# Expert rows of items 0 to 6 kept in DRAM and fetched by token, operand's high part first in five projections, the double norm ordered by norms, the experts' end rotated

## The chip, the cores and the metric

The kernel runs on one core of one Trainium2 chip. The metric is the device time of one execution in microseconds (us). PE is the matmul engine, PEld its weight load, DVE, ACT and POOL the vector, scalar and GpSimd engines, SP the queue that loads the weights.

## The reference, cut to what matters

Three blocks run over 256 tokens of width 1024, all in float32.

```python
def first_block(x, ...):
    h = rmsnorm(x, norm_mix_pre)
    y = mixer(h, w_in, ..., w_out)            # gated conv and gated linear attention
    x = x + rmsnorm(y, norm_mix_post)
    h = rmsnorm(x, norm_ffn_pre)
    y = conv_mlp(h, w_up, conv_ffn, w_down)
    return x + rmsnorm(y, norm_ffn_post)

def moe_swiglu(x, router_w, router_b, w_gate_up, w_down):
    logits = jnp.einsum('td,de->te', xf, router_w) + router_b
    top_v, top_i = lax.top_k(logits, TOP_K)                     # 2 of 8
    gates = jax.nn.softmax(top_v, axis=-1)
    combine = jnp.sum(gates[..., None] * jax.nn.one_hot(top_i, N_EXPERTS), axis=1)
    y = jnp.zeros(xf.shape, F32)
    for e in range(N_EXPERTS):
        y = y + combine[:, e:e + 1] * swiglu(xf, w_gate_up[e], w_down[e])
    return y

def second_block(x, p, ...):
    for i in range(2):
        h = fox_sb_mixer(x, ...) if i == 0 else swa_mixer(x, ...)
        x = layer_norm(DEEPNORM_ALPHA * x + h, ln_mix_g[i], ln_mix_b[i])
        h = swiglu(x, ...) if i == 0 else moe_swiglu(x, ...)
        x = layer_norm(DEEPNORM_ALPHA * x + h, ln_ffn_g[i], ln_ffn_b[i])
        x = x + jax.nn.sigmoid(x @ ple_w_gate[i]) * (p[i] @ ple_w_proj[i])
    return x
```

## The kernel before

**Tiling.** The 256 tokens are two tiles of 128, kept in SBUF as x[tile] of 128x1024. Each projection turns its input first: eight 128x128 transposes for each tile on PE (turn_tile, L2032) into PSUM, of which ACT copies a rounded high part xt_hi (turned, L636) and DVE makes the remainder xt_lo (L1146, rows of L1150). Weights come in chunks of 1 MB, 128x2048, on SP's queue (load, L395) into a ring of raw slots, four of them and during the experts six (w_raw and raw_more). ACT rounds a chunk to w_hi (round_chunk L613, rounds L1049; all of ACT's copies have the line L611), DVE subtracts to w_lo (split_chunk L1138, splits L1701). PE then makes three products for each piece: high by high, the other two with one low part each. A 128x512 product takes some 0.23 us from start to start.

**What sets the order.** Each engine's program is written out by hand: pool from L470, act from L605, dve from L1129, pe from L1905. Engines meet at semaphores. An engine executes in order, so a wait holds whatever is written behind it.

**Operands.** operand(m, src) (L2040) puts in keep_warm products (bf16 of no use, L1998, rows of L2001; BEFORE and BETWEEN at L2003 to L2004 give their numbers), turns tile 0, more warmers, turns tile 1, seven warmers and waits for both tiles' xt_lo (xt_ready). m is 2 for w_up, 3 for ab_in, 5 for ffn_up, 7 for qkv, 9 for the router. The first chunk after it is cols_chunk (L1964, rows of L1976 to L1979) or rows_chunk (L1909, L1922 to L1924); the router's logits are L2575 to L2577.

**The double norm.** After w_out, DVE's rms_after (L1198) makes x of a tile from the projection, and rms_before (L1190) y of the tile from x for w_up's operand; ACT's squares (L678) and square_x (L693) deliver the sums of squares and the roots. The order is tile 0 both, then tile 1 both.

**The sliding-window attention's end.** DVE copies turned probabilities (COPY pt, L1449) that PE multiplies by v (L2413 to L2415), and splits c_out's chunks between.

**Experts.** The router puts up to 128 rows of an expert into an item; eight items run and up to three overflow items for what is left (If blocks on n_items). An item (L1056 ACT, L1724 DVE, L2489 PE) is 28 up-chunks in seven turns of a loop over j, each with four chunks, 48 products and a turn of the hidden rows mh, and 16 down-chunks in two halves: 504 products of 128x512. The rows xg of the next item are prepared beside: DVE's select (L1703) makes sel, the one-hot matrix of tokens against slots, PE turns it (turn_sel, L2471, with the gates' sum of L2476), and the row sum gives row_of (L1745), by which POOL fetches xr from x_rows in DRAM (fetch, L585); PE turns xr in the down part. The item's result, scaled by the gate, is split to ys_hi (ACT) and ys_lo (DVE, L1759), and in the next item PE multiplies it by the turned sel (scatter, L2479, rows of L2485: eight products), so that every row comes to its token, and DVE adds both tiles to y (added, L1713). After the last item come seven warmers, the scatter of the last result, the overflow branches and ple(1): its projection of p (ppt, 24 products for a block), then the norm of y and the turn of x (add_last, L1887), and the gate projection by tiles.

Of the kernel before, what the change touches and what calls it, by code (L numbers as in the profile page):

```python
# [14 lines left out]
ALU = mybir.AluOpType  # L15
ACT = mybir.ActivationFunctionType
F32 = mybir.dt.float32
# [95 lines left out]
MOE_CHUNKS = MOE_UP_CHUNKS + 2 * len(MOE_DOWN)  # L113


def build(nc, a, out, upto="end"):
# [27 lines left out]
    with ExitStack() as ctx:  # L144
# [29 lines left out]
        def S(name):  # L174
# [29 lines left out]
        route_i = sb("route_i", [P, 4], I32)  # L204
        row_of = sb("row_of", [P, 1], U32)
        tok_col = sb("tok_col", [P, NT])
        x_rows = nc.dram_tensor("x_rows", (SEQ + 1, D), F32, kind="Internal").ap()
        at_xt = free[0]
# [54 lines left out]
            ("selt", [P, SEQ], F32R), ("gslot", [P, 1], F32))  # L263
# [21 lines left out]
        def p_bank(i):  # L285

            return psum[:, 2 * (phase["c_out"][0][0] % 2), :] if i else scr[:, 3, :]
# [31 lines left out]
        def last_raw(k, n_items):  # L319
# [3 lines left out]
            return raw_order[at], 16 * (uses - N_EXP * uses_in_item(at)) + 16 * uses_in_item(at) * n_items  # L323
# [64 lines left out]
        def _(sp):  # L388
# [19 lines left out]
            if "moe" in live:  # L408
# [34 lines left out]
                if "ple1" in live:  # L443
                    for _, cc, n0, n, ps in phase["ple1"]:
                        for k, (k0, nk, m) in enumerate(ps, cc):
                            slot, _ = last_raw(k, n_items)
# [23 lines left out]
        def _(pool):  # L470
# [105 lines left out]
            if "moe" in live:  # L576
# [6 lines left out]
                pool.dma_start(x_rows[SEQ:SEQ + 1, :], xr[0:1, :]).then_inc(S("zero_stored"), 16)  # L583

                def fetch(i):  # L585

                    pool.wait_ge(S("row_ready"), i + 1)
# [3 lines left out]
                pool.wait_ge(S("zero_stored"), 16)  # L591
# [13 lines left out]
        def _(act):  # L605
# [7 lines left out]
            def round_chunk(k, r, n):  # L613

                slot, landed = (k % RING, 16 * (k // RING + 1) + 16 * r) if k < N_BEFORE_MOE else last_raw(k, n_items)
# [166 lines left out]
            for t in squares("w_out"):  # L782
                if t == 1:
                    for j in range(2):
                        turned(2, j)
                root_tile(t)
                square_x(t, y, lambda t: act.wait_ge(S("x_tile"), t + 1))
                root_tile(t)

# [160 lines left out]
            def ple(i, m, r=0):  # L950
# [12 lines left out]
                if i:  # L963
                    round_to(blocks[0][1] + RING, r)
                    for block_ in blocks[0:2]:
                        projected(*block_)
                    turned(m, 0)
                    turned(m, 1)
                    root_tile(1)
# [86 lines left out]
            def item(i):  # L1056
                c0, r = N_BEFORE_MOE, i * R_ITEM
                for j in range(MOE_PAIRS):
# [9 lines left out]
                    if j == 2:  # L1068
# [21 lines left out]
            if "moe" in live:  # L1090
# [19 lines left out]
                for i in range(1, N_EXP):  # L1110
                    item(i)
# [1539 lines left out]
```

## Time and profile before

| | us |
|---|---|
| median of 3 runs | 1875.41 (1875.24 to 1876.05) |
| the profiled execution, its own time | 1876.83 |
| span of its profile | 1874.7 |
| PE busy | 1827.1 (97%), 9840 matmuls |
| DVE, ACT busy | 1388.8 (74%), 1105.0 (59%) |
| mean granted clock of PE | 0.991 |

Busy time is the time in which an engine has an instruction under way; matmuls overlap, so a busy PE says that it has something to do, and the distance between two starts says how fast. The granted clock is given as a share of 2.4 GHz, and 0.50 is 1.2 GHz. A bracket behind a row of a timeline gives the idle time before it and what ended it.

### The profile page before, as it was taken

What the parts mean: (1) busy time and instruction counts of PE and PEld (TensorE: products, weight loads), DVE (VectorE), ACT (ScalarE), POOL (GpSimd) and SP (SyncE); (2) the same over time, 40 slices, a digit from 0 to 9 for tenths busy, and PEclk for the clock granted to TensorE, in tenths of its full rate; (3) what the DMA queues carried; (4) which work ended last, traced back from release to release, by engine and by line L of the source; (5) the groups of instructions that cost most, each with busy time, mean ns of one, the idle gap of its engine ahead of it and who ended that gap; (6) DMA issues with size and microseconds to landing.
All of it is one profiled execution on the core that took longest, in us unless ns stands there. A gap on an engine that the chain in (4) does not pass through costs nothing.

```text
span 1874.7 us, 24092 instructions
## 1 busy us (share of the span) xinstructions
PE 1827.1 (97%) x9840; PEld 1527.8 (81%) x9849; DVE 1388.8 (74%) x1200; ACT 1105.0 (59%) x989; POOL 61.6 (3%) x83
## 2 busy tenths in 40 slices
PE   8999999999999999999999999999999999999997
PEld 6979997897899877768788888888888888888875
DVE  4766775456655565689988888888888888888876
ACT  4544554364343344367766676767666767676672
POOL 2200000200000001000000000000000000000000
PEclk8999999999999999999999999999999999999998
DMA  7444546432555563259999999999999999999980
GB/s 252 158 153 157 179 157 213 141 131 100 176 179 179 179 203 136 69 205 384 339 381 361 338 368 352 362 356 342 377 361 340 366 355 362 356 342 379 357 308 24
DMA packets 248857, 491.02 MB, mean 262 GB/s; under 512 B 10423, under 2 KB 15611, under 8 KB 248753
## 3 DMA queue, kind: packets, MB, share of 16 engines
q1 hardware_dynamic: 244992, 477.30, 72.0%
q0 software_dynamic: 3328, 10.73, 1.7%
q8 instruction: 69, 1.13, 0.3%
q10 hardware_dynamic: 432, 1.57, 0.2%
q14 instruction: 36, 0.29, 0.0%
HBM read 487.46 MB, written 2.10 MB: 261 GB/s over the span
## 4 chain that ended last, share of the span: by engine, by line
PE 87%; DVE 7%; ACT 2%; issue 1%; DVEq 1%; DMA 0%; ACTq 0%; SPq 0%
PE psum L2511 17%; PE psum L2513 17%; PE psum L2512 17%; PE psum L1976 5%; PE psum L1979 5%; PE psum L1978 5%; PE psum L1922 5%; PE psum L1923 5%; PE psum L1924 5%; PE psum L1996 3%; DVE w_lo L1138 2%; ACT w_hi L611 1%; DVE w_lo L1701 1%; DVE uv L1398 1%; PE psum L2485 1%
## 5 line engine op out<-in xcount | busy, mean ns | idle before, releaser
L611 ACT ACTIVATE w_hi<-w_raw 128x2048 fp32r<-128x2048 f32 (+1 forms) x357 | 641.4, 1834 | 106.7 <-PE psum L1924 60.3
L1701 DVE TENSOR_TENSOR w_lo<-w_raw,w_hi 128x2048 fp32r<-128x2048 f32 (+1 forms) x238 | 511.3, 2187 | 75.2 <-ACT w_hi L611 75.0
L1138 DVE TENSOR_TENSOR w_lo<-w_raw,w_hi 128x2048 fp32r<-128x2048 f32 (+2 forms) x119 | 261.3, 2227 | 138.9 <-ACT w_hi L611 137.5
L2511 PE MATMUL psum<-w_hi,xg_hi 128*128 128x512 f32 x892 | 357.7, 401 | 1.3 <-DVE w_lo L1701 1.3
L2513 PE MATMUL psum<-w_hi,xg_lo 128*128 128x512 f32 x892 | 353.5, 396 | 0.0
L2512 PE MATMUL psum<-w_lo,xg_hi 128*128 128x512 f32 x892 | 353.5, 396 | 0.0
L1701 DVE TENSOR_TENSOR w_lo<-raw_more,w_hi 128x2048 fp32r<-128x2048 f32 (+1 forms) x118 | 254.5, 2195 | 35.2 <-ACT w_hi L611 35.0
L1976 PE MATMUL psum<-xt_hi,w_hi 128*128 128x256 f32 (+1 forms) x976 | 277.0, 284 | 0.7 <-DVE w_lo L1138 0.7
L1978 PE MATMUL psum<-xt_lo,w_hi 128*128 128x256 f32 (+1 forms) x976 | 274.8, 282 | 0.0
L1979 PE MATMUL psum<-xt_hi,w_lo 128*128 128x256 f32 (+1 forms) x976 | 274.8, 282 | 0.0
L611 ACT ACTIVATE w_hi<-raw_more 128x2048 fp32r<-128x2048 f32 (+1 forms) x118 | 212.7, 1838 | 19.0 <-PE psum L2513 18.5
L2511 PEld LDWEIGHTS psum<-w_hi,xg_hi 128*128 128x128 f32 x892 | 168.1, 188 | 40.9 <-DVE w_lo L1701 2.2
L2513 PEld LDWEIGHTS psum<-w_hi,xg_lo 128*128 128x128 f32 x892 | 167.9, 188 | 40.8
L2512 PEld LDWEIGHTS psum<-w_lo,xg_hi 128*128 128x128 f32 x892 | 168.2, 189 | 38.5
L1976 PEld LDWEIGHTS psum<-xt_hi,w_hi 128*128 128x128 f32 (+1 forms) x976 | 181.8, 186 | 3.5 <-DVE w_lo L1138 1.5
L1978 PEld LDWEIGHTS psum<-xt_lo,w_hi 128*128 128x128 f32 (+1 forms) x976 | 182.6, 187 | 0.5
L1979 PEld LDWEIGHTS psum<-xt_hi,w_lo 128*128 128x128 f32 (+1 forms) x976 | 182.6, 187 | 0.3
L2511 PE MATMUL psum<-w_hi,mh_hi 128*128 128x512 f32 x448 | 179.1, 400 | 0.0
L2513 PE MATMUL psum<-w_hi,mh_lo 128*128 128x512 f32 x448 | 177.6, 397 | 0.0
L2512 PE MATMUL psum<-w_lo,mh_hi 128*128 128x512 f32 x448 | 177.4, 396 | 0.0
L611 ACT ACTIVATE mg<-psum 128x512 f32<-128x512 f32 x56 | 33.6, 599 | 176.1 <-PE psum L2513 176.1
L1922 PE MATMUL psum<-w_hi,xt_hi 128*128 128x512 f32 (+1 forms) x256 | 104.5, 408 | 5.2 <-DVE xt_lo L1150 3.7
(395 smaller groups left out, 2122.9 us busy)
## 6 DMA issues: line engine op xcount, KB each, us to landing
w_raw<-in_moe_w_gate_up SPq DMA_DIRECT2D x150, 1024.0 KB, 7.8
raw_more<-in_moe_w_gate_up SPq DMA_DIRECT2D x74, 1024.0 KB, 7.7
w_raw<-in_moe_w_down SPq DMA_DIRECT2D x64, 1024.0 KB, 7.2
raw_more<-in_moe_w_down SPq DMA_DIRECT2D x32, 1024.0 KB, 7.5
w_raw<-in_w_up SPq DMA_DIRECT2D x22, 1024.0 KB, 5.4
w_raw<-in_ffn_w_gate_up SPq DMA_DIRECT2D x22, 1024.0 KB, 5.4
w_raw<-in_w_in SPq DMA_DIRECT2D x12, 1024.0 KB, 5.6
w_raw<-in_ab_w_in SPq DMA_DIRECT2D x12, 1024.0 KB, 5.2
```

The lines of the kernel that those rows point to most:

```text
L611: return act.activation(o, i, func, **kw)
L1138: TT(w_lo[:, k % RING, 0:n], raw(slot, n), w_hi[:, k % RING, 0:n].bitcast(F32), ALU.subtract)\
L1701: TT(w_lo[:, at, 0:n], raw(slot, n), w_hi[:, at, 0:n].bitcast(F32), ALU.subtract).then_inc(S("lo_ready"), 1)
L1922: mm(o, hi(k, t), wh, start=(k == ps[0][0]), stop=False)
L1923: mm(o, hi(k, t), wl, start=False, stop=False)
L1924: m = mm(o, lo(k, t), wh, start=False, stop=(k == kmax))
L1976: mm(o, w_hi[:, slot, cols], xt_hi[:, k, :], start=(k == 0 and c_ % 2 == 0), stop=False, skip_group_check=True)
L1978: mm(o, w_hi[:, slot, cols], xt_lo[:, k, :], start=False, stop=False, skip_group_check=True)
L1979: m = mm(o, w_lo[:, slot, cols], xt_hi[:, k, :], start=False, stop=(k == KD - 1), skip_group_check=True)
L2511: mm(o, hi[:, q, :], wh, start=(q == first), stop=False)
L2512: mm(o, hi[:, q, :], wl, start=False, stop=False)
L2513: m = mm(o, lo[:, q, :], wh, start=False, stop=(q == last))
```

## The change

1. **Stored rows.** The results of items 0 to 6 (STORED = 7) stay one float32 tile ys, which ACT scales by the gate, and POOL stores it to y_rows in DRAM. Their ys_lo, scatter, additions to y and (for items 1 to 6) the turn of sel are gone; the gate comes as a second column of the row sum. In item 0 DVE computes for each token the two places of its rows (rows_of_tokens); in item 7 POOL fetches them through xr, 512 KB for each tile and choice, and DVE adds them to y. Item 7 and overflow items are scattered as before, but by halves of the columns.
2. **The experts' end rotated.** An item is a head and an end (its last two roundings and the result's second half). The last item's end comes behind the overflow branches, together with ple1's first two chunks, now rounded and split at their true width of 1024; ple1's gate chunks are split behind the norm of the second tile, and the gate projection's first block takes the products with w_hi first (rows_high_first). Warmers before the scatter and before the gate projection are gone, as is the wait for y_added there.
3. **High part first.** At m = 2, 3, 5, 7 and 9 the first chunk starts when xt_hi is there and takes its xt_lo products last; operand puts two warmers there instead of seven and doesn't wait; BETWEEN of w_up is 5 instead of 14. To free the bank for this, p is turned into a free accumulator bank, and so are the logits.
4. **Double norm by norms.** x of both tiles, then y of both tiles, on DVE and ACT.
5. **Attention's end.** The split of one chunk goes from before the last COPY pt to behind it, the next one behind the rows of the last heads.

```diff
@@ POOL
+                def store(i):
+
+                    pool.wait_ge(S("ys_hi_ready"), 2 * i + 2)
+                    pool.dma_start(y_rows[i * P:(i + 1) * P, :], ys[:]).then_inc(S("zero_stored"), 16)
+
+                def fetch_results(g):
+
+                    pool.wait_ge(S("row_ready"), STORED + g)
+                    pool.indirect_dma_start(xr[:], None, y_rows[:], bass.IndirectOffsetOnAxis(ap=token_rows[:, g:g + 1], axis=0))\
+                        .then_inc(S("xr_landed"), 16)
...
-                for i in range(N_EXP):
+                for i in range(STORED):
                     fetch(i)
+                    store(i)
+                pool.wait_ge(S("zero_stored"), 32 + 16 * STORED)
+                pool.wait_ge(S("xr_turned"), STORED)
+                for g in range(2 * NT):
+                    fetch_results(g)
+                fetch(STORED)
@@ ACT
+                if 0 < i < STORED:
+                    act.wait_ge(S("row_ready"), i)
+                if 0 < i <= STORED:
+                    act.wait_ge(S("zero_stored"), 32 + 16 * i)
+                wait_used(act, c0 + end, r)
+                item_rows(i, 0)
+                rounds(end + 2, MOE_CHUNKS, i)
+
+            def item_rows(i, n):
+
+                to = ys if i < STORED else ys_hi
+                copy(to[:, n * NB:(n + 1) * NB], psum[:, 4 + n, :], scale=gslot[:, gate_col(i)]).then_inc(S("ys_hi_ready"), 1)
...
+            def last_end():
+
+                c0 = chunk0["ple1"]
+                round_to(c0 + 2, n_items * R_ITEM)
+                wait_used(act, N_BEFORE_MOE, n_items * R_ITEM)
+                item_rows(ITEMS, 1)
+                round_to(c0 + 4, n_items * R_ITEM)
@@ DVE
             for t in rms_after(1, "w_out", "x_tile"):
+                pass
+            for t in range(NT):
                 rms_before(t, 2)
...
                 swa_sink(1)
-                round_to(c_sw + 7)
                 for t in range(NT):
                     turned_at(8, t, 2 * t, scr[:, t, :])
                 turned_prob(7)
-                round_to(c_sw + 8)
+                round_to(c_sw + 7)
                 attended(1)
...
+                    if i == STORED and 1 <= j <= 4:
+                        add_results(j - 1)
+                    if first and j == MOE_PAIRS - 1:
+                        rows_of_tokens()
...
+            def add_results(g):
+
+                dve.wait_ge(S("xr_landed"), 16 * (STORED + g + 1))
+                TT(y[:, g // 2, :], y[:, g // 2, :], xr[:], ALU.add).then_inc(S("row_ready"), 1)
...
+                last_end()
+                added(n_items, 0)
+                dve.drain()
                 add_last(0)
                 normalize(0, 10, y)
                 add_last(1)
@@ PE
-            BETWEEN = (0, 4, 14, 9, 4, 13, 4, 2, 4, 11, 4)
+            BETWEEN = (0, 4, 5, 9, 4, 13, 4, 2, 4, 11, 4)
...
-                if m not in (6, 10):
-                    keep_warm(7, 3)
-                pe.wait_ge(S("xt_ready"), 4 * (m + 1))
+                keep_warm(2, 3)
...
+            def cols_chunk_high_first(bl, i, r, m_):
...
+                pe.wait_ge(S("xt_hi_ready"), 4 * m_ + (3 if k0 + nk <= 4 else 4))
+                for part in range(2):
+                    if part:
+                        pe.wait_ge(S("xt_ready"), 4 * (m_ + 1))
...
+                            if part:
+                                m = mm(o, w_hi[:, slot, cols], xt_lo[:, k, :], start=False, stop=(k == KD - 1), skip_group_check=True)
+                            else:
+                                mm(o, w_hi[:, slot, cols], xt_hi[:, k, :], start=(k == 0 and c_ % 2 == 0), stop=False,
+                                   skip_group_check=True)
+                                mm(o, w_lo[:, slot, cols], xt_hi[:, k, :], start=False, stop=False, skip_group_check=True)
...
+                high(0, 0)
+                high(1, 0)
+                turn_tile(m, src, 1)
+                low(0, 0)
+                pe.wait_ge(S("xt_ready"), 4 * m + 4)
+                high(0, 1)
+                high(1, 1)
+                low(0, 1).then_inc(S("w_used"), 1)
+                low(1, 0)
+                low(1, 1).then_inc(S("w_used"), 1)
...
-                        if h == 0 and j == 0 and not first and i != N_EXP:
-                            scatter(i)
+                        if h == 0 and j == 0 and i > STORED:
+                            scatter(i, 1)
...
-                keep_warm(7, 0)
-                scatter(N_EXP)
+                scatter(N_EXP, 0)
...
                 overflow(N_EXP)
+                scatter(n_items, 1)
```

What this does to the order of instructions is shown at three places. The first is PE in item 1, at the turn of the third pair's hidden rows; sel is the one-hot matrix. Before:

```order
L2512 MATMUL psum<-w_lo,xg_hi 128x512
L2513 MATMUL psum<-w_hi,xg_lo 128x512
L1996 MATMUL psum<-ident,mh 128x128 x4
L1996 MATMUL psum<-ident,sel 128x128 x2
L2476 MATMUL psum<-route,sel 128x1 x2
L2511 MATMUL psum<-w_hi,xg_hi 128x512
L2512 MATMUL psum<-w_lo,xg_hi 128x512
L2513 MATMUL psum<-w_hi,xg_lo 128x512
```

The change:

```order
L2712 MATMUL psum<-w_lo,xg_hi 128x512
L2713 MATMUL psum<-w_hi,xg_lo 128x512
L2165 MATMUL psum<-ident,mh 128x128 x4
L2711 MATMUL psum<-w_hi,xg_hi 128x512
L2712 MATMUL psum<-w_lo,xg_hi 128x512
L2713 MATMUL psum<-w_hi,xg_lo 128x512
```

The turn of sel and the gates' sum are gone in items 1 to 6, while the turn of mh stands. Item 1's scatter, before, stands like this on PE, behind the second chunk of the item, and nothing is left of it in the change:

```order
L2512 MATMUL psum<-w_lo,xg_hi 128x512
L2513 MATMUL psum<-w_hi,xg_lo 128x512
L2485 MATMUL psum<-ys_hi,selt 128x512
L2485 MATMUL psum<-ys_lo,selt 128x512
L2485 MATMUL psum<-ys_hi,selt 128x512
L2485 MATMUL psum<-ys_lo,selt 128x512
L2485 MATMUL psum<-ys_hi,selt 128x512
L2485 MATMUL psum<-ys_lo,selt 128x512
L2485 MATMUL psum<-ys_hi,selt 128x512
L2485 MATMUL psum<-ys_lo,selt 128x512
L2511 MATMUL psum<-w_hi,xg_hi 128x512
L2512 MATMUL psum<-w_lo,xg_hi 128x512
```

The second place is DVE at the experts' end, from the last item's chunks to the norm (raw_more and w_raw are raw slots, branches are the overflow's). Before:

```order
L1701 TENSOR_TENSOR w_lo<-raw_more,w_hi 128x2048 [waits hi_ready] x2
L1759 SCALAR_TENSOR_TENSOR ys_lo<-psum,gslot,ys_hi 128x512 [waits ys_hi_ready]
L1701 TENSOR_TENSOR w_lo<-w_raw,w_hi 128x2048 [waits hi_ready] x2
L1878 UNCONDITIONAL_BRANCH
L1715 REGISTER_ALU
L1716 TENSOR_TENSOR y<-y,psum 128x1024 [waits scattered]
L1892 BN_STATS bn<-y 128x6 x2
L1234 BN_AGGR stat<-bn 128x2 [waits gain_landed1,gain_landed0]
L1236 TENSOR_SCALAR stat<-stat 128x1
L1239 SCALAR_TENSOR_TENSOR x<-y,stat,gain 128x1024
L1178 RECIPROCAL stat<-stat 128x1 [waits root_ready]
L1241 SCALAR_TENSOR_TENSOR x<-x,stat,gain 128x1024
```

The change:

```order
L2008 UNCONDITIONAL_BRANCH
L1195 ISA
L1197 TENSOR_TENSOR w_lo<-raw_more,w_hi 128x1024 [waits hi_ready]
L1195 REGISTER_ALU
L1197 TENSOR_TENSOR w_lo<-raw_more,w_hi 128x1024 [waits hi_ready]
L1859 REGISTER_ALU
L1844 SCALAR_TENSOR_TENSOR ys_lo<-psum,gslot,ys_hi 128x512 [waits ys_hi_ready]
L1779 TENSOR_TENSOR y<-y,psum 128x512 [waits scattered]
L1779 TENSOR_TENSOR y<-y,psum 128x512
L1776 REGISTER_ALU
L1779 TENSOR_TENSOR y<-y,psum 128x512 [waits scattered]
L1790 BN_STATS bn<-y 128x6
```

Four splits of full width stood ahead of the addition of a whole tile; now two of half width and the result's second half do, behind the branches, and the additions are of 512 columns.

The third is DVE at the end of the sliding-window attention. Before:

```order
L1449 COPY pt_124<-psum 128x768 [waits at_t]
L1443 TENSOR_TENSOR smx_131<-smx_131,sink 128x16
L1138 TENSOR_TENSOR w_lo<-w_raw,w_hi 128x2048 [waits hi_ready]
L1157 TENSOR_TENSOR xt_lo<-psum,xt_hi 128x4x128 [waits xt_hi_ready] x2
L1449 COPY pt_124<-psum 128x768 [waits at_t]
L1138 TENSOR_TENSOR w_lo<-w_raw,w_hi 128x2048 [waits hi_ready]
L1455 TENSOR_TENSOR smx_131<-smx_131 128x16 [waits at_sum]
```

The change:

```order
L1510 COPY pt_125<-psum 128x768 [waits at_t]
L1504 TENSOR_TENSOR smx_132<-smx_132,sink 128x16
L1216 TENSOR_TENSOR xt_lo<-psum,xt_hi 128x4x128 [waits xt_hi_ready] x2
L1510 COPY pt_125<-psum 128x768 [waits at_t]
L1197 TENSOR_TENSOR w_lo<-w_raw,w_hi 128x2048 [waits hi_ready]
L1516 TENSOR_TENSOR smx_132<-smx_132 128x16 [waits at_sum]
L1518 RECIPROCAL smx_132<-smx_132 128x16
```

The copy of pt now has no w_lo between it and the one before.

## Rows read from the trace of the kernel before

**Rows 1.** The page, busy time and the chain.

```profile
PE 1827.1 (97%) x9840; PEld 1527.8 (81%) x9849; DVE 1388.8 (74%) x1200; ACT 1105.0 (59%) x989; POOL 61.6 (3%) x83
...
PE 87%; DVE 7%; ACT 2%; issue 1%; DVEq 1%; DMA 0%; ACTq 0%; SPq 0%
```

**Rows 2.** Tile views of row_of and of xr: duration ns min/median/max, first and last start.

```profile
L1745 DVE TENSOR_SCALAR row_of<-psum x8: 147/148/159, 892.0 to 1764.5; 128x1 uint32<-128x1 f32 x8
...
DMA to landing us min/median/max: 7.2/7.8/8.6
```

**Rows 3.** PE timeline at a scatter: start us, us, engine, line, op, [idle before <-releaser].

```profile
1078.55 0.40 PE L2485 MATMUL psum<-ys_hi,selt 128*128 128x512 f32 x1
...
1080.37 0.40 PE L2511 MATMUL psum<-w_hi,xg_hi 128*128 128x512 f32 x1
```

**Rows 4.** PE timeline at item 1's turn of sel.

```profile
978.81 0.38 PE L1996 MATMUL psum<-ident,sel 128*128 128x128 f32 x2
...
979.39 0.48 PE L2511 MATMUL psum<-w_hi,xg_hi 128*128 128x512 f32 x1
```

**Rows 5.** Windows: us, then busy us PE, PEld, DVE, ACT, POOL, PEclk, DMA share, GB/s.

```profile
830.00:880.00 50.00, 49.32 (x225) 39.75 (x224) 44.13 (x56) 36.32 (x29) 0.00 (x0) 1.00 1.05 387
1124.00:1249.00 125.00, 125.00 (x560) 101.16 (x559) 107.83 (x71) 87.61 (x64) 0.94 (x1) 1.00 1.00 358
```

**Rows 6.** The page, DMA issues: KB, median us to landing.

```profile
x_rows<-x ACTq DMA_DIRECT2D x2, 512.0 KB, 7.4
```

**Rows 7.** PE timeline at w_up's operand.

```profile
140.53 1.97 PE L1996 MATMUL psum<-ident,y 128*128 128x128 f32 x8 [2.65 <-DVEq L1196]
...
144.35 0.47 PE L1976 MATMUL psum<-xt_hi,w_hi 128*128 128x256 f32 x1
```

**Rows 8.** DVE timeline at w_out's double norm.

```profile
135.92 1.28 DVE L1218 SCALAR_TENSOR_TENSOR x<-y,stat,x 128x1024 f32<-128x1024 f32 x1
...
139.16 1.28 DVE L1195 SCALAR_TENSOR_TENSOR y<-x,stat,gain 128x1024 f32<-128x1024 f32 x1
```

**Rows 9.** PE timeline at ab_in's operand.

```profile
346.08 1.67 PE L2001 MATMUL psum<-ones_tri 128*128 128x512 bf16 x7
347.83 0.39 PE L1976 MATMUL psum<-xt_hi,w_hi 128*128 128x256 f32 x1
```

**Rows 10.** DVE and PE timelines at the sliding-window attention's end.

```profile
770.50 2.29 DVE L1138 TENSOR_TENSOR w_lo<-w_raw,w_hi 128x2048 fp32r<-128x2048 f32 x1
...
774.91 0.43 PE L2413 MATMUL psum<-p,pt 128*128 128x64 f32 x2 [2.34 <-DVE pt L1449]
...
782.31 0.60 PE L1996 MATMUL psum<-ident,y 128*128 128x128 f32 x4
```

**Rows 11.** PE and DVE timelines at the router.

```profile
808.38 1.09 PE L1996 MATMUL psum<-ident,x 128*128 128x128 f32 x8 [1.42 <-DVEq L1242]
...
811.99 2.29 DVE L1811 TENSOR_TENSOR xn_lo<-x,xn_hi 128x2048 fp32r<-128x2048 f32 x1 [0.17 <-ACT xn_hi L611]
814.95 0.17 DVE L1815 TENSOR_TENSOR route<-psum,rb_row 128x16 f32<-128x16 f32 x1 [0.67 <-PE psum L2581]
```

**Rows 12.** Windows with the granted clock at 0.50.

```profile
775.24:782.06 6.82, 6.82 (x22) 5.77 (x22) 3.54 (x5) 0.21 (x1) 0.92 (x1) 0.50 0.82 279
1836.78:1847.02 10.24, 4.87 (x15) 3.41 (x17) 9.21 (x16) 3.57 (x8) 0.00 (x0) 0.50 0.01 2
```

**Rows 13.** PE and DVE timelines of the experts' end and ple1.

```profile
1828.08 0.50 PE L1922 MATMUL psum<-w_hi,ppt_hi 128*128 128x512 f32 x1 [1.89 <-issue]
...
1833.56 0.39 PE L1924 MATMUL psum<-w_hi,ppt_lo 128*128 128x512 f32 x1
1841.93 1.97 PE L1996 MATMUL psum<-ident,x 128*128 128x128 f32 x8 [7.98 <-DVEq L1242]
...
1869.73 0.40 PE L1924 MATMUL psum<-w_hi,xt_lo 128*128 128x512 f32 x1
...
1835.88 1.22 DVE L1716 TENSOR_TENSOR y<-y,psum 128x1024 f32<-128x1024 f32 x1 [3.05 <-issue]
```

More of the change, by code:

```diff
@@ L1109, in _ @@
                 n_items = act.value_load(route_i[0:1, 3:4], min_val=N_EXP, max_val=ITEMS)
-                for i in range(1, N_EXP):
+                n_over = act.value_load(route_i[0:1, 4:5], min_val=0, max_val=ITEMS - N_EXP)
+                for i in range(1, N_EXP - 1):
                     item(i)
+                item_head(N_EXP - 1)
                 def overflow(i):
                     with act.If(n_items > i):
-                        item(i)
+                        item_end(i - 1)
+                        item_head(i)
                         if i + 1 < ITEMS:
@@ L1383, in _ @@
             for t in rms_after(1, "w_out", "x_tile"):
+                pass
+            for t in range(NT):
                 rms_before(t, 2)
@@ L1729, in item @@
                         lo_h(i, j - 1)
-                    elif not first:
+                    elif i > STORED:
                         scattered(i)
@@ L1885, in _ @@
                 me.cap = N_STATIC
[L1887 to L1892 removed]
+                last_end()
+                added(n_items, 0)
+                dve.drain()
                 add_last(0)
@@ L2471, in turn_sel @@
             def turn_sel(n):
-                for t in range(NT):
+                for t in range(NT if n else 0):
                     turn(psum[:, 4, t * P:(t + 1) * P], sel[:, t, :].bitcast(F32))
@@ L2477, in turn_sel, with scatter @@
                 m.then_inc(S("sel_turned"), 1)
-            def scatter(n):
-                pe.wait_ge(S("ys_ready"), 2 * n)
+            def scatter(n, h):
+                pe.wait_ge(S("ys_ready"), 2 * n - 1 + h)
                 for t in range(NT):
-                    for h in range(2):
-                        for q, part in enumerate((ys_hi, ys_lo)):
-                            m = mm(psum[:, 4 + 2 * t + h, :], selt[:, t * P:(t + 1) * P], part[:, h * NB:(h + 1) * NB],
-                                   start=(q == 0), stop=(q == 1))
-                    m.then_inc(S("scattered"), 1)
+                    for q, part in enumerate((ys_hi, ys_lo)):
+                        m = mm(psum[:, 4 + 2 * t + h, :], selt[:, t * P:(t + 1) * P], part[:, h * NB:(h + 1) * NB],
+                               start=(q == 0), stop=(q == 1))
+                m.then_inc(S("scattered"), 1)
             def item(i, first=False):
```

279 lines of the change are left out of this document (194 added, 85 removed).

## The prediction

> **What bounds the kernel now.** I read the page first: PE is busy for 1827.1 of the span's 1874.7 us, and 87% of the chain that ended last is PE's [rows 1]. So a matmul that disappears is worth its start-to-start distance, and work of other engines is worth nothing unless PE waits for it. Then the tile view of row_of and xr [rows 2]: one row_of per expert item, eight in all, from 892.0 to 1764.5, so an item takes (1764.5 - 892.0) / 7 = 124.64 us. Eight fetches also say that no overflow item runs. Next the windows: in a whole item PE is busy all 125 us, DVE 107.8, ACT 87.6 [rows 5]: PE sets the pace there. Last the timelines at the boundaries between stages, where PE does wait, and the windows in which the granted clock is 0.50, that is 1.2 GHz [rows 7 to 13].
>
> **Experts, rows stored.** In each of items 1 to 7 stand eight scatter products, in item 2 from 1078.55 to the next weight product at 1080.37 [rows 3]: 1.82 us. Before, seven of these stand inside the items (the eighth is in the tail, below): 7 x 1.82 = 12.7 us gone. The turn of sel with its gate products runs from 978.81 to 979.39 [rows 4], 0.58 us; items 1 to 6 lose it, 3.5 us, and item 0 loses its two turns, some 0.2. The row sum only gets a second column. Sum 16.4 us, all on the path, because PE has no idle time to fill there.
>
> What is added lies beside PE, if the others keep up:
> - **DVE** loses two ys_lo and two y additions in an item and gains twelve small operations in item 0 and four additions of 128x1024 in item 7. One such addition takes 1.22 us [rows 13]. A turn of the item's loop over four up-chunks has 48 products of some 0.24 us (24 ppt products run from 1828.08 to 1833.80, [rows 13]), 11.5 us, and DVE fills 107.8 / 125 = 86% of an item [rows 5], here 9.9: with 1.22 more it is at 11.1, so it fits with 0.4 us to spare. That is thin, and each addition waits for a fetch.
> - **The fetches** of item 7 go one after the other through xr: each takes 7.8 us to landing [rows 2] and about one more for its issue, against one addition every 11.5 us. They fit.
> - **DMA.** An item loads 44.04 MB of weights and 0.52 of rows, and now stores 0.52: 45.1 MB in 122.3 us is 369 GB/s; with four fetches for item 7's additions 386. The trace shows 358 in a whole item, which is just the demand (44.56 / 124.64), and 387 over the 50 us of 830 to 880, where the six slots are being filled [rows 5]. So 369 is inside what was seen and 386 at its edge. I charge 0.4 us for items 0 and 7 together and take 16.0; bounds 12 (item 7 short of data by 4 us) and 17.2 (the turn's pipeline refill also saved).
>
> The nearest rule against this: the Trainium skill, "DMA: Bandwidth & Descriptors", section "Where 436 GB/s comes from", says that for HBM to SBUF the HBM side, about 358 GB/s for a core, binds. By that the 45.1 MB need 126 us, items 1 to 7 get longer instead of shorter, and the total is some 1867. The trace disagrees with its 387 over 50 us.
>
> **Operand's high part first.** At w_up, ab_in, ffn_up, qkv and the router, five of seven warmers go, and the first products need only the turned high part. At ab_in the seven warmers stand between 346.08 and 347.83 [rows 9]: 5/7 of 1.75 is 1.25 us. The pieces at ffn_up and qkv read the same: 3 x 1.25 = 3.75 us. The two left are 0.5 us and the ACT copies of the turn end about when they do, so nothing new waits; bound below 0.6 each (ACT late), above 1.45. At the router the logits come 1.3 us earlier, but DVE's 2.29 us operation at 811.99 stands ahead of the step that reads them at 814.95 [rows 11], which can only start at 814.3: 0.65 us; bounds 0 and 1.3. w_up is in the next part.
>
> **Double norm by norms.** Before, tile 0's second norm (3.1 us with its wait for ACT) stands ahead of tile 1's first. x of tile 1 is ready at 135.92 + 1.28 = 137.2, y of tile 1 at 139.16 + 1.28 = 140.44, of which 1.96 is waiting for ACT's squares and root [rows 8]. Norm by norm x of tile 1 comes at about 133.8, ACT's squares of tile 0 are hidden under it, and the two y end at about 136.7 and 138.75. Tile 0's turn gets some 3 us later and tile 1's, which decides, 1.7 earlier (140.53 to 138.8) [rows 7]. PE then idles some 3 us before turn 0. Here the gap of 2.65 us before turn 1 was followed by a turn of 1.97 us, and one of 2.34 at 774.91 by the window at 0.50 [rows 7, 10, 12], so I take turn 1 and two warmers at half speed, 1.8 and 0.9 us: first product at 141.4 instead of 144.35. That is 3.0 us with the fewer warmers in it; bounds 2.0 (more products at half clock) and 4.3 (no fall).
>
> **End of the sliding-window attention.** DVE makes a 2.29 us w_lo at 770.50, ahead of the copy pt [rows 10]; PE waits 2.34 us for pt, and from 775.24 to 782.06 its clock is 0.50 [rows 10, 12]. Without that w_lo the copy waits for ACT's xt_hi instead, pt is ready 1.3 us earlier, PE's gap is 1.0 us; one of 1.42 at the router left the turn behind it at 1.09 us, full speed [rows 11]. The 18 small and 12 large products from 774.91 to 782.31 took 7.4 us; at full clock the 12 large ones take 12 x 0.24 = 2.8, the small ones 1.35, with the earlier start 773.6: y's turn at 777.75. The moved w_lo ends at 775.8 and y at about 777.7, so they don't hold it. Gain 4.6 us; 2.3 if the clock falls all the same.
>
> **Experts' end.** Before: the scatter's eight products end at 1826.2, behind seven warmers that now go; 1.89 us for the branches, 24 ppt products to 1833.8, while DVE works off four 2.2 us splits, waits and only adds at 1835.88; the turn of tile 0 is at 1841.93, after 7.98 us of idle PE; the last product starts at 1869.73 [rows 13]. After: the first half is scattered at 1822.4, straight behind the last expert product, and added under the branches, the second half at 1825.4, DVE adds it at 1826.45, having before it only two splits of half width. From DVE's addition to the turn it was 6.05 us, less 0.5 for the half addition: turn 0 at 1832.0, 9.9 us earlier, just where the ppt products now end. From that turn to the last product's end before: 28.0 us, five warmers and a turn at half clock among them. After, DVE's normalization of tile 1 ends at 1839.2 and the first w_lo at 1841.5; PE waits 2.5 us for the turned operand (1832.9 to 1835.4), does high products of tile 0, waits about 1.0 for w_lo: about 28.1 again. That is 9.8, and the 2.5 us gap is of the size that brought the clock down, for 6.8 us at 774 and for 10.2 in the tail before [rows 12]. A 6.8 us stretch costs up to 3.4 us: I take the middle, 8.1. Bounds 5 and 9.8.
>
> **Sum.** 16.0 + 3.75 + 0.65 + 3.0 + 4.6 + 8.1 = 36.1 us. The profiled execution took 1876.8, so 1840.7 for it; the median of the runs shown is 1875.41, 1.4 lower, and 1875.4 - 36.1 = **1839.3**. All low ends together: 12 + 1.8 + 0 + 2.0 + 2.3 + 5 = 23, 1852; all high ones: 17.2 + 4.35 + 1.3 + 4.3 + 4.6 + 9.8 = 41.6, 1834.
>
> **Rivals.**
> - *The warmers are missed.* Fourteen go at w_up and five at each other place, and PE has 1.0 to 2.5 us gaps with fewer products around. A stretch like 775.24 to 782.06 [rows 12] costs half of its 6.8 us; two or three of them 7 to 10: about 1848. Against: the gap of 1.42 us at the router wasn't followed by a fall [rows 11]. Chance 0.08.
> - *Item 7 starves, or DVE falls behind.* 386 GB/s, a serial chain of fetches, DVE with 0.4 us to spare: 5 to 10 us, 1844 to 1849. For: DVE's high share [rows 5]. Chance 0.09.
> - *Transfers can do no more than the 358 GB/s of the whole items*, whose DMA share is already 1.00 [rows 5]: 45.1 MB take 126.0 us, 3.7 more than planned, seven times: 26, so 1865. Against: the 387 (share 1.05) and that 358 equals the demand. (The Trainium skill's rule above would act like this.) Chance 0.05.
> - *The other side: each new transfer stops the weight stream.* If the weights stand still for the whole landing time of a store (7.4 us for 512 KB, [rows 6]) or fetch (7.8), 7 x 7.4 + 4 x 7.8 = 83 us: 1922. It decides for slower from (36.1 + 3.75) / 11 = 3.6 us of PE time per transfer. Against: today's fetch of xr takes 7.8 us in each item and PE has no idle time in it [rows 2, 5]. Chance 0.03.
> - *It doesn't do what it says*: a token beyond an expert's 128 rows would go the old way; eight fetches say there is none. With the stores' wait in front of ACT's copy of the next item's rows PE could stall, but a store has over 100 us. Chance 0.01, near 1856.
>
> **How the numbers follow.** The forecast's own mechanism has 0.74. The range holds its bounds and the first two rivals: 1832 (two below the high sum, for what I have not seen) to 1853; outside are the capped transfers, the blocked stream and the failed change, 0.09, and some 0.06 of misjudged sizes. What a measurement can tell from no change is 0.2%, 3.75 us, 1871.7 to 1879.2. Only the blocked stream lies above; a mild form of it lies within: faster 0.96, same 0.01, slower 0.03.
>
> **What would show it.** Row_of's pitch falls from 124.64 to 122.3 with PE busy all the time in a window of an item; ys stores land in under 10 us; no PE wait for DVE or ACT above 0.5 us in item 7; the 0.50 window at 775 is gone and one near 137 to 142 remains; at the experts' end no idle PE stands before turn 0, and 2.5 us behind it. A pitch that stays near 124.6, or weight loads landing later than 9 us, would make the prediction wrong; so would more than 43 us from the first ppt product to the span's end (now 1874.7 - 1828.1 = 46.6, forecast 40).

## The result and the profile after

The change takes 1828.19 us (median of 4, 1827.59 to 1830.17) against 1875.73 for the kernel before (4 runs), a ratio of 0.9747 with the 95% interval 0.973 to 0.9764. It is faster, as forecast, but by 47.5 us instead of 36.1, and below the range of 1832 to 1853. The profiled execution has a span of 1826.2.

The page of the changed kernel: busy time, granted clock, chain, and DMA issues (KB each, median us to landing).

```profile
PE 1783.6 (98%) x9701; PEld 1502.2 (82%) x9708; DVE 1369.5 (75%) x1198; ACT 1099.7 (60%) x976; POOL 73.7 (4%) x95
...
PEclk8999999999999999999999999999999999999999
...
PE 87%; DVE 7%; ACT 2%; issue 1%; DVEq 1%; DMA 0%; ACTq 0%; SPq 0%
...
w_raw<-in_moe_w_gate_up SPq DMA_DIRECT2D x150, 1024.0 KB, 9.1
```

The shape is that of [rows 1]: 98% busy PE, and PE has 87% of the chain. The same row of the kernel before:

```profile
w_raw<-in_moe_w_gate_up SPq DMA_DIRECT2D x150, 1024.0 KB, 7.8
```

So the weight loads land later, 9.1 us after issue instead of 7.8. The prediction had named more than 9 us as a sign of being wrong. It came, and nothing followed from it: in a whole item PE is busy all the time, with 373 GB/s where [rows 5] have 358.

```profile
1124.00:1249.00 125.00, 125.00 (x560) 101.58 (x560) 107.55 (x69) 87.13 (x62) 1.54 (x2) 1.00 1.01 373
138.03:141.44 3.41, 3.41 (x14) 2.30 (x13) 2.57 (x5) 1.21 (x3) 0.53 (x1) 0.50 0.33 108
1786.66:1790.08 3.42, 3.42 (x10) 2.67 (x9) 2.63 (x6) 1.98 (x3) 0.00 (x0) 0.50 0.04 16
```

(Columns as in [rows 5].) Only two stretches at 0.50, 1.2 GHz, are left between the start and the end, each 3.4 us: one at w_up's turn, one behind the branches at the experts' end. That is 6.8 us, where the kernel before has 23.9 us. The two of [rows 12] are gone. The item's pitch, from the tile view of row_of:

```profile
L1827 DVE TENSOR_SCALAR row_of<-psum x8: 148/152/159, 873.9 to 1726.4; 128x1 uint32<-128x1 f32 x8
```

(1726.4 - 873.9) / 7 = 121.79 us, where 122.3 was forecast. PE at w_up's operand, at the attention's end and at the experts' end:

```profile
136.66 1.09 PE L2165 MATMUL psum<-ident,y 128*128 128x128 f32 x8 [3.56 <-DVEq L1255]
...
139.28 1.91 PE L2165 MATMUL psum<-ident,y 128*128 128x128 f32 x8
...
141.46 0.47 PE L2125 MATMUL psum<-xt_hi,w_hi 128*128 128x256 f32 x1
```

```profile
761.49 0.43 PE L2613 MATMUL psum<-p,pt 128*128 128x64 f32 x2 [1.05 <-DVE pt L1510]
...
765.73 0.60 PE L2165 MATMUL psum<-ident,y 128*128 128x128 f32 x4
```

```profile
1785.74 0.49 PE L2685 MATMUL psum<-ys_hi,selt 128*128 128x512 f32 x1 [1.99 <-DVE ys_lo L1844]
...
1793.92 1.04 PE L2165 MATMUL psum<-ident,x 128*128 128x128 f32 x8
1796.61 0.49 PE L2513 MATMUL psum<-w_hi,xt_hi 128*128 128x512 f32 x1 [1.65 <-DVE xt_lo L1209]
...
1802.47 1.20 PE L2520 MATMUL psum<-w_lo,xt_hi 128*128 128x512 f32 x4 [1.01 <-DVE w_lo L1197]
...
1821.21 0.40 PE L2049 MATMUL psum<-w_hi,xt_lo 128*128 128x512 f32 x1
```

The first answers to [rows 7]: a gap of 3.56 us, turn 1 at half clock, the first product at 141.46, where 141.4 was forecast. The second answers to [rows 10]: the wait for pt is 1.05 us instead of 2.34. The third answers to [rows 13]: no wait before turn 0, then 1.65 and 1.01 us, where 2.5 and 1.0 were forecast.

So where do the missing 11 us lie? Landmarks of both traces (start times in us), how far the change is ahead at each, and how far the forecast's terms up to there would have it:

```
                       before    after     ahead   forecast
first w_up product     144.35    141.46     2.9      3.0
last w_down product    341.25    335.96     5.3      3.0
first ab_in product    347.83    341.30     6.5      4.3
first ffn_up product   487.25    478.74     8.5      5.5
last ffn_down product  675.66    665.25    10.4      5.5
y's turn, attention    782.31    765.73    16.6     11.4
first expert product   822.44    804.99    17.5     12.0
last expert product   1822.13   1782.43    39.7     28.0
last product          1869.73   1821.21    48.5     36.1
```

At the boundaries between stages the steps are near those of the forecast. The rest comes inside stages that nothing of the change touches: 1.9 us in ffn_up and ffn_down alone. There the products simply follow each other faster. The mean distance from one start to the next, over all weight products of a stage at full clock, is 0.2342 us before and 0.2328 after for 128x512, 0.1200 and 0.1188 for 128x256, from the first 100 us on. 128x512 products of ppt, the turned p, alone have 0.234 in both. All operands but ppt's lie behind the one new declaration in SBUF, token_rows, which moves them by 32 bytes.

### The profile page after: what moved, and what is told of

Its sections match the earlier page's. It is cut to its first block, busy times and chain, and to the rows that moved or that the text cites. A ratio compares the mean times of both kernels' runs of the same rounds, so it can differ in the third digit from the quotient of the medians.

```text
span 1826.2 us, 23845 instructions
## 1 busy us (share of the span) xinstructions
PE 1783.6 (98%) x9701; PEld 1502.2 (82%) x9708; DVE 1369.5 (75%) x1198; ACT 1099.7 (60%) x976; POOL 73.7 (4%) x95
## 4 chain that ended last, share of the span: by engine, by line
PE 87%; DVE 7%; ACT 2%; issue 1%; DVEq 1%; DMA 0%; ACTq 0%; SPq 0%
PE psum L2711 16%; PE psum L2713 16%; PE psum L2712 16%; PE psum L2047 5%; PE psum L2049 5%; PE psum L2048 5%; PE psum L2142 5%; PE psum L2144 4%; PE psum L2145 4%; PE psum L2165 3%; DVE w_lo L1197 2%; DVE w_lo L1762 1%; ACT w_hi L641 1%; PE psum L2125 1%; PE psum L2127 1%
## 5 line engine op out<-in xcount | busy, mean ns | idle before, releaser
L1197 DVE TENSOR_TENSOR w_lo<-w_raw,w_hi 128x2048 fp32r<-128x2048 f32 (+2 forms) x121 | 265.7, 2228 | 133.5 <-ACT w_hi L641 132.0
L1762 DVE TENSOR_TENSOR w_lo<-raw_more,w_hi 128x2048 fp32r<-128x2048 f32 (+1 forms) x116 | 250.1, 2195 | 35.6 <-ACT w_hi L641 35.4
L2142 PE MATMUL psum<-xt_hi,w_hi 128*128 128x256 f32 (+2 forms) x768 | 217.8, 284 | 1.0 <-DVE w_lo L1197 1.0
L2144 PE MATMUL psum<-xt_lo,w_hi 128*128 128x256 f32 (+2 forms) x768 | 216.7, 282 | 0.0
L2145 PE MATMUL psum<-xt_hi,w_lo 128*128 128x256 f32 (+2 forms) x768 | 216.6, 282 | 0.0
L2142 PEld LDWEIGHTS psum<-xt_hi,w_hi 128*128 128x128 f32 (+2 forms) x768 | 143.5, 187 | 3.2 <-DVE w_lo L1197 1.9
L2144 PEld LDWEIGHTS psum<-xt_lo,w_hi 128*128 128x128 f32 (+2 forms) x768 | 143.5, 187 | 0.5
L2145 PEld LDWEIGHTS psum<-xt_hi,w_lo 128*128 128x128 f32 (+2 forms) x768 | 143.5, 187 | 0.3
L2713 PEld LDWEIGHTS psum<-w_hi,mh_lo 128*128 128x128 f32 x448 | 84.4, 188 | 19.9
```

Source lines behind the costliest of these rows:

```text
L1197: TT(w_lo[:, k % RING, 0:n], raw(slot, n), w_hi[:, k % RING, 0:n].bitcast(F32), ALU.subtract)\
L1762: TT(w_lo[:, at, 0:n], raw(slot, n), w_hi[:, at, 0:n].bitcast(F32), ALU.subtract).then_inc(S("lo_ready"), 1)
L2142: mm(o, w_hi[:, slot, cols], xt_hi[:, k, :], start=(k == 0 and c_ % 2 == 0), stop=False, skip_group_check=True)
L2144: mm(o, w_hi[:, slot, cols], xt_lo[:, k, :], start=False, stop=False, skip_group_check=True)
L2145: m = mm(o, w_lo[:, slot, cols], xt_hi[:, k, :], start=False, stop=(k == KD - 1), skip_group_check=True)
L2713: m = mm(o, lo[:, q, :], wh, start=False, stop=(q == last))
```

## The experiments

### The place of the operands

Four runs ask whether the 32 bytes do it (theory P in the expectations). Rival R is that the distance differs from one execution or chip to the next, rival C that it comes with the program's code. The kernel before again, for its trace:

> The kernel before, word for word, for its trace alone. The step of the forecast in question: products of 128x512 start every 0.2341 us in the trace before and every 0.2327 in the trace after, from the first stage on, where nothing of the change has run yet. Theory P (the place of the operands: 32 bytes more in front of the turned operand in the change): 0.2341 again. Rival R (the rate differs from one execution or chip to the next): anything between 0.232 and 0.235. It also shows whether the half clock at w_down (290.5 to 294.0, behind a gap of 2.75 us) comes again; in the change it did not come behind a gap of 2.86.

The kernel before with 32 and with 64 bytes left free behind tok_col (and, in the same way, 96 below):

```diff
         tok_col = sb("tok_col", [P, NT])
+        free[0] += 32
```

> The kernel before with 32 bytes left free in front of the turned operands and all that lies behind them, no instruction changed. Theory P: 128x512 products start every 0.2327 us instead of 0.2341 and 128x256 ones every 0.1187 instead of 0.1200, that is 9 to 10 us in all: 1866, ratio 0.995. Rival R, and rival C (the rate comes with the program's code): 0.2341 and 1875.5, ratio 1.000.

> The same with 64 bytes. Theory P, if what counts is whether the operands lie at a multiple of 64 bytes (before they don't, in the change they do): 0.2341 and 1875.5, ratio 1.000. If any other place than the one of before were as good, 1866. Rival R: as b_pad32.

The change, with the operands back where they were:

```diff
-        row_of = sb("row_of", [P, 1], U32)
-        token_rows = sb("token_rows", [P, 2 * NT], U32)
+        rows_u = sb("row_of", [P, 1 + 2 * NT], U32)
+        row_of, token_rows = rows_u[:, 0:1], rows_u[:, 1:1 + 2 * NT]
```

> The changed kernel with token_rows in the 32 bytes that row_of takes anyway, so that the operands lie where they lay before; instructions as in the change. Theory P: 0.2341 and about 10 us more than the change's 1828.2: 1838, ratio to before 0.980. Rivals R and C: 1828, ratio 0.9747.

Measured: the kernel before again (b_again) has 0.2342 and one run of 1877.5, and its clock falls at the same place in w_down. b_pad32 took 1862.9, ratio 0.9934 (0.9921 to 0.9947), b_pad64 1867.2, 0.9951 (0.9938 to 0.9964), with distances of 0.2326 and 0.2335. a_back32 took 1840.1, 0.9808 (0.9795 to 0.9821), with 0.2342. The rows of row_of in b_pad32, b_pad64 and a_back32:

```profile
L1746 DVE TENSOR_SCALAR row_of<-psum x8: 149/152/159, 885.8 to 1752.6; 128x1 uint32<-128x1 f32 x8
```

```profile
L1746 DVE TENSOR_SCALAR row_of<-psum x8: 151/152/159, 885.9 to 1755.8; 128x1 uint32<-128x1 f32 x8
```

```profile
L1827 DVE TENSOR_SCALAR row_of<-psum x8: 147/148/155, 880.7 to 1737.8; 128x1 uint32<-128x1 f32 x8
```

Pitches of 123.83 and 124.27 against 124.64 of [rows 2], and 122.44 against the change's 121.79. No instruction differs between the kernel before and b_pad32 or b_pad64, nor between the change and a_back32. Rivals R and C are out: the same distance comes back with the same place, 0.2342 in all four traces that have the old one, whatever the code, on two chips. b_pad32 gained 13.3 us, where 9 to 10 were expected from the distance; its trace also has 13.7 us at 1.2 GHz between the start and the end instead of 23.9, and why is not shown. And what the change does by itself, at the old place, is 36.1 us: 1876.2 - 1840.1.

That leaves open how the distance runs over the places, and what it is that has to lie well. The same edit with 64, 96, 128, 160 and 192 bytes in the change (a_pad64 to a_pad192), whose operands lie at 32 already, gives places 96 to 224; b_pad96 is the kernel before at place 96; a_base64 moves everything:

> The changed kernel with 64 more bytes in front of the turned operands, 96 beyond where they lay before. So far 128x512 products start every 0.2341 us at the old place, 0.2327 at 32 beyond, 0.2335 at 64 beyond. If the places repeat after 64 bytes, 96 is as good as 32: 0.2327 and 1828, ratio 0.9747. If each of the four places in 128 bytes has its own rate, it may be any of 0.2325 to 0.2341, 1826 to 1838. If the change's own place gives the rate by something else (the code), 1828 as well.

> The changed kernel with the operands 128 bytes beyond where they lay before. If the places repeat after 128 bytes: the old rate, 0.2341, and 1838 to 1840, ratio 0.981, as with the operands at the old place itself. If it is only the old place that is bad, or the rates are chance: 0.2327 to 0.2335 and 1828 to 1834.

> The changed kernel with everything in SBUF, the weights' slots too, 64 bytes further; the operands stand to the weights as in the change. If what counts is how operand and weights stand to each other: 0.2327 and 1828. If the operand's own place counts: the rate of the run with 64 more bytes. If the weights' own place counts, another one; it could also be better than any so far, 1820.

```diff
-        free = [-(-nc.sbuf_base // 64) * 64]
+        free = [-(-nc.sbuf_base // 64) * 64 + 64]
```

> The kernel before with 96 bytes left free in front of the turned operands, no instruction changed. The changed kernel at this place started a 128x512 product every 0.2290 us and took 1803.3. If the place alone does that: 0.2290, and the 8376 weight products (half of them of 256 columns, 0.1152 instead of 0.1200) save about 36 to 38 us: 1839. If it needs the change's code: 0.234 and 1875. With it the change itself, both kernels at their best place, would be worth 1839 - 1803 = 36 us, as the forecast's sum had it.

> The changed kernel with the operands 160 bytes beyond the old place. If the rate repeats after 128 bytes, as at 32: 0.2328 us for a 128x512 product and 1828. If not, a rate of its own; so far 0: 0.2342, 32: 0.2328, 64: 0.2335, 96: 0.2290, 128: 0.2332.

> The same at 224 bytes beyond the old place. If the rate repeats after 128 bytes, as at 96: 0.2290 and 1803. If 96 is good for another reason: 0.2328 to 0.2342 and 1828 to 1840.

> The changed kernel with the operands 192 bytes beyond the old place. So far, us for a 128x512 product: 0: 0.2342, 32: 0.2328, 64: 0.2335, 96: 0.2290, 128: 0.2332, 160: 0.2275, 224: 0.2332. If odd multiples of 32 are the good ones (but 224), 0.2333 here; otherwise its own rate.

a_pad64 took 1803.3, 0.9607 (0.9591 to 0.9623): 25 us less than the change, for 64 bytes left free. a_pad96 took 1829.0 (0.9746, 0.9729 to 0.9762), a_base64 1829.1 (0.9751, 0.9735 to 0.9767). b_pad96, the old code at a_pad64's place, took 1840.1, 0.9816 (0.9795 to 0.9837), forecast 1839; against it the change is worth 36.8 us. (Of the weight products 3000, about a third, have 256 columns, and not half as the expectation has it.) Single runs: a_pad128 1806.7, a_pad160 1823.9, a_pad192 1827.9. All places, in bytes behind that of the kernel before:

```
place              0      32      64      96      128     160     192     224
128x512 us      0.2342  0.2328  0.2335  0.2290  0.2332  0.2275  0.2333  0.2332
128x256 us      0.1200  0.1188  0.1183  0.1150  0.1183  0.1200  0.1167  0.1175
```

(The column for 32 is the change's; b_pad32 has 0.2326 and 0.119 there.) The distances don't repeat after 64 or 128 bytes, and the two shapes have different good places. Places 32 and 96, and 160 for 128x512, were traced more than once, the others beyond 0 once each. The row of row_of in a_pad64 and a_pad128, pitches of 120.06 and 119.34:

```profile
L1828 DVE TENSOR_SCALAR row_of<-psum x8: 144/146/151, 862.9 to 1703.3; 128x1 uint32<-128x1 f32 x8
```

```profile
L1828 DVE TENSOR_SCALAR row_of<-psum x8: 146/148/150, 871.4 to 1706.8; 128x1 uint32<-128x1 f32 x8
```

a_base64 says that it is the place of operand and weights to each other, for the one shift of both that was tried: there everything but ppt moves by 64 bytes, and the experts' products keep 0.2328, where an operand moved alone by 64 bytes (a_pad64) has 0.2290. The products of ppt, whose place is counted from the end of SBUF and whose weights moved, now have 0.2329 instead of 0.234. The first and the last of 24 ppt products of ple0 on PE, with one turn of eight among them, in the change and in a_base64:

```profile
665.48 0.40 PE L2047 MATMUL psum<-w_hi,ppt_hi 128*128 128x512 f32 x1
...
671.74 0.40 PE L2049 MATMUL psum<-w_hi,ppt_lo 128*128 128x512 f32 x1
```

```profile
665.24 0.40 PE L2047 MATMUL psum<-w_hi,ppt_hi 128*128 128x512 f32 x1
...
671.46 0.40 PE L2049 MATMUL psum<-w_hi,ppt_lo 128*128 128x512 f32 x1
```

6.26 and 6.22 us, about what 23 distances shorter by 0.0012 make. The same stretch takes 6.25 to 6.26 us in all the other traces, in which neither ppt nor its weights move: it is their control. Why some places are better stays open; nothing in these traces shows what the loads of one operand and the stream of the other meet in.

### What the parts are worth

The attention's end alone, in the kernel before:

```diff
-                round_to(c_sw + 7)
                 for t in range(NT):
                     turned_at(8, t, 2 * t, scr[:, t, :])
                 turned_prob(7)
-                round_to(c_sw + 8)
+                round_to(c_sw + 7)
```

> The kernel before with one edit alone: DVE's split of one chunk moved behind the last copy of pt. By the forecast PE's wait for pt falls from 2.34 to 1.0 us, the clock does not fall there, and y's turn stands 4.6 us after-start earlier: 1871, ratio 0.9975. If the clock falls all the same, 2.3 us: 1873.2. Rival: the chunk's w_lo, now late, or y holds PE: 0 to 1 us.

1872.5 us, 0.9981 (0.9972 to 0.9991): 1.7 to 5.3 us less, which holds both the 4.6 us forecast and the 2.3 us for a clock that falls all the same. The trace decides, and its clock does not fall there:

```profile
770.68 0.43 PE L2412 MATMUL psum<-p,pt 128*128 128x64 f32 x2 [1.05 <-DVE pt L1449]
...
774.93 0.60 PE L1995 MATMUL psum<-ident,y 128*128 128x128 f32 x4
```

From the last turn of s_more to y's turn it is 5.6 us, before 10.0: 4.4 of the 4.6 forecast.

The double norm back to the order by tiles, in the change (the same in ACT's squares):

```diff
             for t in rms_after(1, "w_out", "x_tile"):
-                pass
-            for t in range(NT):
                 rms_before(t, 2)
```

> The changed kernel with the double norm tile by tile again, on DVE and ACT. By the forecast tile 1's y then comes 1.7 us later, turn 1 at 140.5 instead of 139.3 and the first product at 143.2 instead of 141.5: 1829.9 against 1828.2. Rival: with fewer warmers the clock at turn 1 decides, and the order of the norms is worth less than 0.5 us.

One run of 1828.1. Its operand:

```profile
139.92 1.75 PE L2163 MATMUL psum<-ident,y 128*128 128x128 f32 x8 [4.59 <-DVEq L1255]
...
141.96 0.78 PE L2123 MATMUL psum<-xt_hi,w_hi 128*128 128x256 f32 x1
```

From the warmers before turn 0 (130.83 here, 131.42 in the change) to the first product it is 11.1 us against 10.0, and the clock stays at 0.50 until 143.6. So the order by norms is worth 1.1 us at the first product and under one more behind it, as the products until 143.6 run at half clock: most of the 1.7 expected. The time of the whole does not show it: one run of 1828.1 against the change's 1828.2, where 1829.9 was expected.

More warmers before that turn, at a_pad64's place (a_warm, BEFORE of w_up 20 instead of 8):

> The changed kernel at the 96 byte place, and 20 warmers instead of 8 before the turn of w_up's tile 0, where PE idles 3.56 us in the change and the clock then falls to 0.50 for turn 1 and the warmers behind. If the gap makes the clock fall: none there, turn 1 takes 1.04 instead of 1.9 us and the first product comes 1.2 us earlier: 1802.1 against 1803.3. Rival: the wait is DVE's y, and the first product waits for it whatever the clock: no difference.

```profile
133.84 1.09 PE L2166 MATMUL psum<-ident,y 128*128 128x128 f32 x8 [0.97 <-DVEq L1256]
...
137.38 0.36 PE L2126 MATMUL psum<-xt_hi,w_hi 128*128 128x256 f32 x1
```

The gap shrinks to 0.97 us, the clock stays, and from tile 0's turn to the first product it is 3.54 us instead of a_pad64's 4.71: the 1.2 us are there in the trace. The time, 1802.3 (0.9609, 0.9592 to 0.9626), can't be told from a_pad64's.

Each store made twice, in the change (the waits for the stores count both; not shown):

```diff
                     pool.dma_start(y_rows[i * P:(i + 1) * P, :], ys[:]).then_inc(S("zero_stored"), 16)
+                    pool.dma_start(y_again[i * P:(i + 1) * P, :], ys[:]).then_inc(S("zero_stored"), 16)
```

> The changed kernel with each of the seven stores of 512 KB made twice, to two places in DRAM, and ACT's wait for both. Theory: the stores lie beside PE, which stays busy: 1828 to 1829. Rival of the forecast (a transfer stops the weight stream for its landing time, or the demand meets a cap of transfers): 7 x 3 to 7 us more, 1849 to 1877.

1827.5 us, 0.9748 (0.9731 to 0.9764): no cost that can be told from nothing. The page's DMA issues and windows of two items:

```profile
y_rows<-ys POOLq DMA_DIRECT2D x7, 512.0 KB, 6.5
y_again<-ys POOLq DMA_DIRECT2D x7, 512.0 KB, 8.7
```

```profile
1124.00:1249.00 125.00, 125.00 (x561) 101.54 (x561) 107.59 (x69) 87.91 (x63) 2.08 (x3) 1.00 1.01 376
1249.00:1374.00 125.00, 125.00 (x560) 101.54 (x559) 106.11 (x69) 90.51 (x63) 2.08 (x3) 1.00 1.01 376
```

The second store takes 8.7 us to land, loads and stores together carry 376 GB/s for 250 us on end, and PE has no idle time. That is above the 358 of the rule that the prediction weighed. The Trainium skill's "HBM Reference", Specifications (TRN2), says that this figure is a core's share when both cores of a memory domain stream, and that one alone measures about 425. The kernel runs on one core, and its 376 agree as far as they go: they lie above the share, and no run here comes near 425.

### The best version

> The changed kernel with the projections' operands (xt) 96 bytes beyond the old place and the phase's operands (the experts' xg and mh, ht, ya) 160 beyond, and 20 warmers before w_up's turn. If each operand's own place counts: 0.2275 us for the experts' products instead of 0.2290, some 5000 products, 7 us, and 0.115 for the 256 column ones: 1795. If one place rules both: no better than 1802. If it is the sum of SBUF in use or chance: between 1802 and 1828.

```diff
         tok_col = sb("tok_col", [P, NT])
+        free[0] += 64
...
-        at_phase = at_xt + 2 * nbytes([P, KD, SEQ])
+        at_phase = at_xt + 2 * nbytes([P, KD, SEQ]) + 64
...
-            BEFORE = (0, 10, 8, 0, 18, 0, 4, 0, 18, 0, 24)
+            BEFORE = (0, 10, 20, 0, 18, 0, 4, 0, 18, 0, 24)
```

1794.9 us, 0.9565 (0.9547 to 0.9582), where 1795 was expected: the experts' operands at place 160 have 0.2274 for 128x512, the projections' at place 96 have 0.1148 for 128x256, each as if alone. It beats both kernels, the change by 33 us.

```profile
L1828 DVE TENSOR_SCALAR row_of<-psum x8: 147/148/152, 861.6 to 1698.2; 128x1 uint32<-128x1 f32 x8
```

## Why the prediction was wrong

**The step that failed** is in the sum, and unspoken: "a matmul that disappears is worth its start-to-start distance", with that distance held fixed for all matmuls that stay. The sum has no term for them, so it put their change at nothing, without a reason. 8376 weight products stay, and the distance shrinks by 0.0012 to 0.0014 us. That gives 1.9 us in ffn_up and ffn_down, some 0.65 us in each item (122.44 - 121.79), and by 8376 x 0.0013 at most 10.9 us in all. The spans of a_back32 and the change show some 9 of it (1838.3 - 1826.2, less 3 for the clock, below). It comes from 32 bytes in front of the operands, a line of the diff that the prediction didn't weigh. With the operands at the old place the change measures 1840.1, and 1839.3 was forecast.

**The clock** makes up the rest, and with both signs. In the kernel before, w_down has 3.4 us at 0.50 behind a gap of 2.75 us and loses 1.7 us; in the change a gap of 2.86 at the same place is followed by full clock. Before, the row behind the gap and the window at 0.50:

```profile
289.28 0.47 PE L1922 MATMUL psum<-w_hi,ht_hi 128*128 128x512 f32 x1 [2.75 <-DVE w_lo L1138]
...
290.54:293.96 3.42, 3.42 (x10) 2.65 (x9) 3.42 (x3) 0.74 (x1) 0.00 (x0) 0.50 0.93 331
```

The change:

```profile
285.92 0.48 PE L2047 MATMUL psum<-w_hi,ht_hi 128*128 128x512 f32 x1 [2.86 <-DVE w_lo L1197]
```

In a_back32 the stretch at 0.50 came earlier and cost less. But there the clock fell at the router too, as the rival "the warmers are missed" has it. The change has the same instructions and no fall there, and the gaps before that place are the same within 0.05 us, so it is not shown that the missing warmers are the cause. a_back32's window and the 32 products of its gather:

```profile
805.13:815.37 10.24, 10.24 (x42) 9.37 (x41) 5.52 (x4) 7.11 (x5) 0.00 (x0) 0.50 0.26 74
```

```profile
804.72 3.48 PE L2668 MATMUL psum<-sel,xn_hi 128*128 128x128 f32 x16
808.00 3.62 PE L2668 MATMUL psum<-sel,xn_lo 128*128 128x128 f32 x16
```

The same products in the change, at full clock:

```profile
801.28 2.08 PE L2668 MATMUL psum<-sel,xn_hi 128*128 128x128 f32 x16
803.20 1.95 PE L2668 MATMUL psum<-sel,xn_lo 128*128 128x128 f32 x16
```

The gather took 6.7 us in a_back32, and from the logits to the first expert product it is 14.9 us against 11.9 in the change. So the hit of 36.1 for a_back32 is luck in part: it holds a loss of 3 us that was not forecast and gains of about as much. Two of its five runs have a mean clock of 0.993 instead of 0.991 and took 1837.8 and 1839.4.

**Point by point**, in a_back32, where nothing but the change's own steps differs from before (us gained, the forecast in brackets): w_up 2.7 (3.0; some 0.4 us more lies before it, in the start); ab_in 1.25, ffn_up 1.37, qkv 1.58 (1.25 each); the attention's end 4.4 (4.6); the logits 1.37 earlier, and of it 0.75 left at the first expert product in the change (0.65). The experts 16.8 (16.0): the full price of scatter and sel, and neither fetches nor additions held PE in item 7; the charge of 0.4 was not needed. The tail 8.6 (8.1): turn 0 came without a wait as forecast, but 11.6 us behind the last expert product, where the forecast's times make 9.9. The clock fell for 3.4 us, not at the gap that was named but at one of 2.10 us (1.99 in the change) behind the branches, where PE waited for ys_lo, and the ppt products ran into it. Behind turn 0 PE waited 1.65 us instead of 2.5, and the clock stayed.

The first product of w_up at 141.46 is a hit by two misses of about half a us each. In the change y of tile 1 was ready at 138.67 as forecast, but the five warmers in front of turn 1 ran at half clock and held it until 139.28 instead of 138.8; the two warmers behind took 0.5 us instead of 0.9. Of the rivals, the caps of transfers and the blocked stream are refuted by a_store2, and item 7 didn't starve. For the cap the prediction gives two totals, 1867 and 1865; 1839.3 + 26 is 1865, and nothing else rests on it.

## What to carry to other kernels

Before a sum of removed instructions is trusted to a few tenths of a per cent, compare where the operands lie in SBUF. Here a new 4-element tensor ahead of them was worth some 9 us, and 64 bytes of padding 25 us, more than any single part of the change. So try some paddings of 32 bytes for each large operand once the order of work stands, and when two versions are compared, compare them at the same place. And take the distance between two products from both traces, in a stage that the change doesn't touch, before any step is credited with the difference.

## What was not expected of the hardware

- The distance of 128x512 float32 products runs from 0.2275 to 0.2342 us, 2.9%, over eight places of the operand to the weights in steps of 32 bytes, and that of 128x256 from 0.1148 to 0.1200, 4.5%. bf16 warmers have 0.216 (median) in every trace.
- Which gap is followed by a fall of the granted clock is not told by its length alone: 2.86 us (the change, w_down) were not, 2.75 (before, w_down) and 1.99 (the change, behind the branches) were, and of two routers with the same instructions one (a_back32) had 10.2 us at 1.2 GHz.
- 376 GB/s of loads and stores over 250 us (a_store2), with 8.7 us for the landing of the second store, left PE busy throughout.
